# Sixteen weight buffers as one ring in order of use, with four experts in the loop's body

## What is computed

```python
logits = xt @ w_router + b_router              # 256 tokens, 32 experts
top_logits, top_idx = lax.top_k(logits, 4)
top_w = softmax(top_logits)
# for each expert e, on the tokens that chose it:
gate, up = split(xb @ w_gu[e] + b_gu[e])       # w_gu[e]: 1024 x 2048
gate = minimum(gate, 7.0)
up = clip(up, -7.0, 7.0)
act = (up + 1) * (gate * sigmoid(1.702 * gate))
y = act @ w_dn[e] + b_dn[e]                    # w_dn[e]: 1024 x 1024
# y, weighed by top_w, is added at the token's place
```

## Time and profile before

| | |
|---|---|
| median of three runs | 2118.11 us (2112.33 to 2120.79) |
| the profiled execution | 2111.71 us, span 2110.0 us |
| PE matmuls busy | 1948.9 us, 92% of the span, 10917 records |
| PE weight loads busy | 1222.1 us, 10918 records |
| DVE, ACT, POOL busy | 908.0, 469.5, 70.5 us |
| gate/up matmuls (L1182) | 459.2 us in a group of 2048, 597 ns each |
| down matmuls (L1220) | 192.5 us in a group of 864, 594 ns each |
| DMA | 581.37 MB, mean 276 GB/s |

### The profile page before, as it was taken

One profiled execution on the slowest core, in us unless ns is written; L12 is line 12 of the kernel. 1 busy time (PEld: TensorE's weight loads), 2 busy tenths in 40 slices (PEclk: granted clock), 3 DMA queues, 4 the chain that ended last, 5 costly groups with the idle time before them and its releaser, 6 DMA issues. The chain is left out here.

```text
span 2110.0 us, 28553 instructions
## 1 busy us (share of the span) xinstructions
PE 1948.9 (92%) x10917; PEld 1222.1 (58%) x10918; DVE 908.0 (43%) x1444; ACT 469.5 (22%) x557; POOL 70.5 (3%) x128
## 2 busy tenths in 40 slices
PE   4999896999999999999999999989999998999998
PEld 2859774433333333333333333358987997878986
DVE  3799644111111111111111121176556787876554
ACT  2223101000000000100000000024543643334542
POOL 2000002000000000000000000010000000020000
PEclk9999997999999999999999999999999989999999
DMA  9794834959999999899999985936555620054552
GB/s 360 246 324 156 300 126 146 417 216 422 421 422 422 422 422 422 332 423 422 422 422 422 408 344 226 401 107 213 180 198 164 202 96 1 1 173 162 189 190 80
DMA packets 143604, 581.37 MB, mean 276 GB/s; under 512 B 10520, under 2 KB 12552, under 8 KB 94281
## 3 DMA queue, kind: packets, MB, share of 16 engines
q1 hardware_dynamic: 136384, 564.43, 68.6%
q0 software_dynamic: 3040, 11.02, 1.7%
q10 hardware_dynamic: 4105, 4.86, 0.7%
HBM read 579.23 MB, written 1.05 MB: 275 GB/s over the span
## 5 line engine op out<-in xcount | busy, mean ns | idle before, releaser
L1182 PE MATMUL bank<-ring,area 128*64 128x512 f32 x2048 | 459.2, 597 | 28.0 <-DMA ring<-in_w_gu 27.6
L1182 PEld LDWEIGHTS bank<-ring,area 128*64 128x64 f32 x2048 | 144.0, 137 | 325.3 <-issue 235.5
L924 PE MATMUL bank<-area_r,ring_r 128*128 128x256 f32 x992 | 282.6, 285 | 9.3 <-DVE area_r L2155 7.1
L926 PE MATMUL bank<-area_r,ring_r 128*128 128x256 f32 x992 | 281.5, 284 | 0.0
L927 PE MATMUL bank<-area_r,ring_r 128*128 128x256 f32 x992 | 281.5, 284 | 0.0
L289 DVE TENSOR_TENSOR ring_r<-ring,ring_r 128x2048 fp32r<-128x2048 f32 x90 | 205.8, 2291 | 149.8 <-ACT ring_r L286 148.1
L2420 DVE TENSOR_SCALAR area<-bank 128x512 f32<-128x512 f32 x36 | 24.9, 692 | 539.6 <-PE bank L1182 539.6
L286 ACT ACTIVATE ring_r<-ring 128x2048 fp32r<-128x2048 f32 x92 | 175.7, 1913 | 179.4 <-PE bank L927 152.2
L924 PEld LDWEIGHTS bank<-area_r,ring_r 128*128 128x128 f32 x992 | 191.3, 193 | 12.1 <-DVE area_r L2155 7.3
L1220 PE MATMUL bank<-area 128*64 128x512 f32 x864 | 192.5, 594 | 0.6 <-DVE area L2434 0.5
L926 PEld LDWEIGHTS bank<-area_r,ring_r 128*128 128x128 f32 x992 | 191.3, 193 | 0.0
(11 more groups left out here) (341 smaller groups left out, 2177.8 us busy)
## 6 DMA issues: line engine op xcount, KB each, us to landing
ring<-in_w_gu SPq DMA_DIRECT2D x256, 1024.0 KB, 21.1
area<-in_w_dn SPq DMA_DIRECT2D x96, 1024.0 KB, 21.0
ring<-in_mlp_w SPq DMA_DIRECT2D x64, 1024.0 KB, 5.4
ring<-in_w_dn SPq DMA_DIRECT2D x32, 1024.0 KB, 19.5
ring<-in_w_in SPq DMA_DIRECT2D x24, 1024.0 KB, 6.3
ring<-in_gdn_w_in SPq DMA_DIRECT2D x16, 1024.0 KB, 5.5
area<-in_w_mod SPq DMA_DIRECT2D x12, 1024.0 KB, 8.6
ring<-in_w_mod SPq DMA_DIRECT2D x8, 1024.0 KB, 17.1
```

The lines of the kernel that those rows point to most:

```text
L924: ins = mm(out_, a_[0], b_[0], start=start, stop=False)
L926: mm(out_, a_[0], b_[1], start=False, stop=False)
L1182: ins = mm(bk[hf * BLK:(hf + 1) * BLK, :], x(kt), block_u[:, c:c + BANK], start=False, stop=kt == ND - 1)
```

## The change

The sixteen slots become one ring: unit u of the j-th expert of a group has slot (12 j + u) mod 16, and the loads are issued in the order of use, an expert's gate/up units first and its down units after them. 48 units, those of four experts, are three turns of the ring, so the loop's body has to hold four experts (`EG = 4`) for slots to be constants in the code. What was done once per group of two is now done once per pair (`EPAIR = 2`): the gather's halves, the slots, the staged copy. PE gets one more wait, on the staged copy of the expert before, at the third expert of a group. The loads behind the experts wait for other counts: the side input and `pool_scale` for the last expert's eight gate/up units, the four first units of the stream for the slots that they take now.

```diff
-EG = 2
+EG = 4
+EPAIR = 2
...
-        GU_SLOTS = tuple(range(NGU))
-        DN_SLOTS = ((8, 9, 10, 11), (12, 13, 14, 15))
...
-        ER = NU + len(DN_SLOTS[1])
+        ER = 16
+        assert EG * NU % ER == 0
...
         def expert_slot(j, u):
-            return GU_SLOTS[u] if u < NGU else DN_SLOTS[j][u - NGU]
+            return (NU * j + u) % ER
 
         def expert_landed(g, j, u):
             earlier = pre_loads[expert_slot(j, u)]
-            if u < NGU:
-                return g * (16 * EG) + 16 * (earlier + j + 1)
-            return g * 16 + 16 * (earlier + 1)
-
-        load_order = [(0, u) for u in range(NGU)] + [(0, u) for u in range(NGU, NU)]
-        for e in range(1, NE):
-            load_order += [(e, u) for u in range(NGU, NU)] + [(e, u) for u in range(NGU)]
+            return g * (16 * (EG * NU // ER)) + 16 * (earlier + (NU * j + u) // ER + 1)
+
+        load_order = [(e, u) for e in range(NE) for u in range(NU)]
...
-            return 16 * (pre_loads[slot_of(n)] + NE + (n - PRE) // RING2 + 1)
+            return 16 * (pre_loads[slot_of(n)] + NE * NU // ER + (n - PRE) // RING2 + 1)
...
-        PE = Steps(moe_pe, (PE_MAIN, PE_MAIN), PE_OVER, 3)
-        DV = Steps(moe_dve, (DVE_FIRST, DVE_MAIN), DVE_OVER, 2)
-        AC = Steps(moe_act, (ACT_FIRST, ACT_SECOND), ACT_OVER, 3)
+        PE = Steps(moe_pe, (PE_MAIN, PE_MAIN) * (EG // EPAIR), PE_OVER, 3)
+        DV = Steps(moe_dve, (DVE_FIRST, DVE_MAIN) * (EG // EPAIR), DVE_OVER, 2)
+        AC = Steps(moe_act, (ACT_FIRST, ACT_SECOND) * (EG // EPAIR), ACT_OVER, 3)
...
-                    sp.wait_ge(w_used, PRE + NU * (NE - 1) + s + 1)
+                    sp.wait_ge(w_used, PRE + NU * NE - ER + s + 1)
...
-            sp.wait_ge(w_used, PRE + NU * (NE - 1))
+            sp.wait_ge(w_used, PRE + NU * (NE - 1) + NGU)
...
-            pool.wait_ge(w_used, PRE + NU * (NE - 1))
+            pool.wait_ge(w_used, PRE + NU * (NE - 1) + NGU)
...
+                half_ = j % EPAIR
                 if j == 0:
                     AC.did(pe, (w[0], EG - 1, 0), "staged_in", pairs_ago=1)
-                gate_and_up(w, lambda kt: xg[kt // UK][:, kt % UK, j * BLK:(j + 1) * BLK], True)
+                elif half_ == 0:
+                    AC.did(pe, (w[0], j - 1, 0), "staged_in")
+                gate_and_up(w, lambda kt: xg[kt // UK][:, kt % UK, half_ * BLK:(half_ + 1) * BLK], True)
                 AC.started(pe, w)
                 scatter(spread_T, y_blk).then_inc(w_used, 1)
-                if j == 0:
+                if half_ == 0:
                     DV.did(pe, w, "next_slots3")
-                gather_pair(bX, j)
+                gather_pair(bX, half_)
...
-                if isinstance(w[2], int) and w[1] == EG - 1:
+                if isinstance(w[2], int) and w[1] % EPAIR == EPAIR - 1:
                     f(xg[0], xg_staged, ACT.Copy).then_inc(moe_act, 1)
...
-                if j == 0:
-                    for i in range(EG):
-                        find_slots(slots[:, :, i * BLK:(i + 1) * BLK], e + (EG + i), 0)
+                if j % EPAIR == 0:
+                    for i in range(EPAIR):
+                        find_slots(slots[:, :, i * BLK:(i + 1) * BLK], e + (j + EPAIR + i), 0)
...
-                copy_tokens(xg_staged if j == 0 else xg[1])
+                copy_tokens(xg_staged if j % EPAIR == 0 else xg[1])
```

More of the change, by code:

```diff
@@ L662, in _ @@
                 s = expert_slot(e % EG, u)
+                assert s == n % ER
                 if n >= ER:
@@ L2435, in copy_act_T @@
                                        bk[:, 0:256].rearrange("p (j s) -> p j s", s=P)))
-            for e in range(EG):
+            for e in range(EPAIR):
                 for t in range(NT):
```

## The result

| | before | after |
|---|---|---|
| median of four runs | 2117.73 us | 2232.47 us (2227.58 to 2233.85) |
| span of the profiled execution | 2110.0 us | 2229.5 us |
| first to last sigmoid (L1790) | 991.6 us | 1105.5 us |
| last sigmoid to the span's end | 738.6 us | 745.7 us |
| packets on q8 | 54 | 136 |

The changed kernel is slower: ratio 1.0541, 95% interval [1.0513, 1.0568]. The forecast was 2145, and its range ended at 2174. The sign and the mechanism were right, the size was not. In the kernel after, L1163, L1171, L1182, L1220, L648, L676, L678 and L817 of before are L1160, L1168, L1179, L1217, L644, L673, L675 and L814; L1790, L2401, L2408, L2485 and L2494 kept their numbers.

The account below looks back on a forecast made before the run. Transfers at 422 GB/s or PE's own work took turns as the limit. Cold code +66.1, waiting -40.8, loop heads -1.3, stage end +3 gave +27 on 2118.11: 2145 us; range 2118 - 22 to 2118 + 56.

Parts of the forecast that it names:

- What bounds the kernel: Expert loop: PE's own work, 26.6 us an expert, where weights are at hand; otherwise transfers at 422 GB/s, 29.82 us.
- the size of the reserve: Landed weight units PE lives on after each transfer stop: they covered 17.3 and 16.7 us, growing by 9.9 us.
- 19.8 + 1.3: Expert loop: 19.8 us less waiting from loading in order of use, 1.3 us from fewer loop heads.
- 15.1 us of waiting at 3.25: Experts 3 to 15: 15.1 us of waiting left in place of 25.0; transfers fall 3.25 us behind PE per expert.
- The code doesn't stay: PE's loop: four experts' code, over 8.9 packets in place of 4.4, doesn't fit and is fetched anew each pass.
- the likeliest case: PE's loop code fetched anew at 6 to 12.6 us a pass: +4 to +57 us, chance 0.50.
- The price of a pass in cold code: PE's loop: one entry and three crossings, 8.9 us a pass, bounds 0 and 12.6; eight passes 71.5 us.
- 1.77: PE's gap in us between experts 0 and 1 in the first pass, taken for each of three crossings per pass.
- The forecast's bound: Turn of PE's loop: two packets needed in a row, another 3.63 us, so 12.6 us a pass.
- The end of the stage: After the last expert: SP's later loads cross pool_w and pool_b and delay the first eviction, +3 us, bounds 0 and 9.
- The rival with resident code: PE's loop code is fetched once and kept: -18 us, 2100 us; chance 0.25.
- the mostly hidden one: PE's loop code is fetched anew but PE pays only the turn, 3.63 us each: -10.5 us, 2108 us; chance 0.20.

Follow-up runs that it names:

- the pair whose code stays: The changed kernel without the extra-block code of every second expert, and the kernel before with the same cut: 2053.12 us and 2076.62 us.

## Why the prediction was wrong in size

- **What bounds the kernel**, and the size of the reserve: right. In the pair whose code stays the ring gave 19.3 us in the beats, against 19.8 + 1.3 forecast, and its slow stretch before expert 16 lasts five experts, where 15.1 us of waiting at 3.25 are 4.6.
- **The code doesn't stay.** Right, and the likeliest case. The trace of before couldn't give the limit, and this was said; it lies between 6.9 and 7.7 packets, where the body after has 9.3.
- **The price of a pass in cold code**: this step failed. It was put at 8.9 us with 12.6 as its bound, and measured 20.2: 157.7 us between the sigmoids and 3.6 at the first entry make 161.3 over eight passes, in place of 71.5. Three things were missed.
  1. The jump into the fourth expert costs 5.5 us, not 1.77. The kernel before crosses only from its first expert to its second and back to the head, so its first pass had no row for this place. The 1.77 was carried over to a jump that it hadn't measured; the run without the fourth expert's extra block (26.4 in the beat) and expert 27, which runs its own (30.7), show that it is the jump which costs.
  2. The turn costs 10.5 us, not 3.63 or twice that. The forecast's bound had two packets in a row, but at the price of the loop's first entry, which was a poor stand-in: there the sequencer comes from straight code, and part of the fetch may have been covered (not shown). In windows of 0.1 us q8 has a packet at 508.9, at 514.6 and at 517.8 us; PE ends at 509.6 and restarts at 520.1. This reads as two fetches, one after the other, at 5.7 and 5.5 us, the first begun 0.7 us before PE stops; the third packet is one fetched ahead. Ahead of the fourth expert the packet is at 475.7 us and PE restarts at 481.3: one such fetch, 5.6 us. The Trainium skill ("Runtime: NRT & Kernel Launch", Instruction fetch mechanics) says that a taken branch to a page outside the current window of two waits for the fetch; the trace agrees on the wait, with 5.5 to 5.7 us a fetch, though not on the two.
  3. After such a gap PE runs at the 1.2 GHz level for 3 us and more. The forecast had no term for it. The beats at the seven turns and the seven fourth experts grew by 36 us more than the gaps there (142.9 against 106.7), 2 to 3 us each, which is about half of the time at the lower level.
- **The end of the stage**: right in kind and inside its bounds (0 to 9), but put at 3 where the eviction is 5.6 later and the rest of the kernel 7.1 longer. From issue to landing pool_b took 6.5 us before and 12.1 after: 5.6 more, where half share was put at 4 more.
- **The sum, put right**: the forecast of +27 with 161.3 for 71.5 (+89.8) and 7.1 for 3 (+4.1) gives +121; the profiled executions differ by 119.5.
- **The range** had its upper bound from the first pass of the kernel before, the only rows for cold code. A first pass shows the fetches of that code at those places; it bounds nothing for a body with other jumps. The rival with resident code fell with the 136 packets, the mostly hidden one with the price of the turn: it had 3.63 us there, and 10.5 were measured.

## What to carry to other kernels

Before a loop's body grows, count the instructions of the engine's program in it, the branches that are seldom taken included, and hold them against what is known to stay: once over the limit, all of a loop's code was fetched again on every turn here, and a copy of seldom used code can be what tips it. A jump that leads out of the fetched code cost up to two fetches in series, and the stops of the matmuls cost clock on top; neither could be bounded from code that runs straight on. Moving the seldom used code behind the loop took back the whole loss, but the entries into it cost most of what the ring gives; the waits that a change moves at the end of a stage are worth a look of their own.

## What was not expected of the hardware

- PE's code cost is a step, not a slope: 204 instructions more in a body of 1760, none of them run, made 54 us (2053.12 to 2107.17) and took q8 from 2 packets to 63 between 480 and 1340 us.
- A fetch that PE waits for takes 5.5 to 5.7 us from its packet to the restart or to the next packet, though the packet takes 1.1 us on the DMA engine (four packets with 1.9% of 16 engines in 15 us).
- A gap of 5.5 us was enough for the granted clock to be 0.50 when PE starts again, and it stayed there for 3 us of busy matmuls, 5 after the gap of 10.5.
- A hint at the back edge took 2.4 us off the gap at the turn (10.47 to 8.06) while its target had to be fetched.
